# A two-block transformer kernel: the hybrid mixers' convolution tiles, value tiles and convolution norm in another order

## The reference, cut to what matters

```python
def hybrid_mixer(h, cos, sin, w_in, q_a_norm, w_uq, kv_a_norm, w_ukv, conv_w,
                 attn_out_norm, conv_out_norm, w_o):
    proj = h @ w_in          # 1024 -> 384 + 256 + 32 + 512 + 512 + 512
    c_q, c_kv, k_pe, gate_b, gate_c, val = jnp.split(proj, offs, axis=-1)
    q = (rms_norm_2(c_q, q_a_norm) @ w_uq)      # 8 heads of 64 + 32 (rotated)
    kv = (rms_norm_2(c_kv, kv_a_norm) @ w_ukv)  # 8 heads of 64 keys + 64 values
    ...                                         # k_pe is rotated and shared by the heads
    attn = causal_attention(q_full, k_full, v)
    conv = gate_b * causal_short_conv(gate_c * val, conv_w)   # 3 taps along the tokens
    merged = concatenate([rms_norm_2(attn, attn_out_norm), rms_norm_2(conv, conv_out_norm)])
    return merged @ w_o
```

## Time and profile before

| what | value |
|---|---|
| median of three runs | 3661.96 us |
| the profiled execution's own time | 3659.31 us |
| its span, first to last instruction | 3657.5 us |
| mean granted TensorE clock | 0.989 of full speed |
| TensorE (PE) busy | 3585.8 us, 98% |
| VectorE (DVE) busy | 2027.3 us, 55% |
| ScalarE (ACT) busy | 1296.0 us, 35% |

### The profile page before, as it was taken

The page is one execution under the profiler, slowest core; times in us unless marked ns, Lnnn a source line. Parts: engine busy times, 40 slices in busy tenths (PEclk is TensorE's granted clock), DMA queues, the critical chain, the costliest instruction groups (busy, mean ns, idle before and its releaser), DMA issues. The chain is left out here.

```text
span 3657.5 us, 46530 instructions
## 1 busy us (share of the span) xinstructions
PE 3585.8 (98%) x17492; PEld 2883.4 (79%) x17492; DVE 2027.3 (55%) x3405; ACT 1296.0 (35%) x2116; POOL 57.2 (2%) x108
## 2 busy tenths in 40 slices
PE   8999999999999999999999998999999999989999
PEld 7777777888866788888888776888888887778887
DVE  5777776655766565575334656433443346564334
ACT  4545444222243332223233433322332234333232
POOL 0000000000000000000000000000000000000000
PEclk9999999999999999999999998999999999989999
DMA  4222212655511265552222211222222322212232
GB/s 140 73 73 76 73 62 104 217 177 198 173 58 47 81 214 187 185 196 91 95 96 93 78 62 58 91 98 98 92 92 98 98 92 69 70 52 94 95 99 81
DMA packets 141561, 386.22 MB, mean 106 GB/s; under 512 B 21424, under 2 KB 62768, under 8 KB 141392
## 3 DMA queue, kind: packets, MB, share of 16 engines
q1 hardware_dynamic: 126928, 306.39, 25.4%
q0 software_dynamic: 14464, 77.60, 6.2%
HBM read 381.85 MB, written 2.10 MB: 105 GB/s over the span
## 5 line engine op out<-in xcount | busy, mean ns | idle before, releaser
L1079 PE MATMUL psP<-h_hi,w_hi 128*128 128x512 f32 x2664 | 1061.3, 398 | 6.1 <-ACT h_hi L689 3.0
L1080 PE MATMUL psP<-h_hi,w_lo 128*128 128x512 f32 x2664 | 1038.9, 390 | 0.0
L1084 PE MATMUL psP<-h_lo,w_hi 128*128 128x512 f32 x2664 | 1028.8, 391 | 0.0
L1692 DVE TENSOR_TENSOR w_lo<-raw,w_hi 128x1024 fp32r<-128x1024 f32 (+1 forms) x465 | 557.8, 1200 | 378.4 <-ACT w_hi L649 371.8
L655 ACT ACTIVATE ybuf<-psP 128x512 f32<-128x512 f32 (+1 forms) x401 | 239.4, 597 | 1276.9 <-PE psP L1084 1276.4
L1079 PEld LDWEIGHTS psP<-h_hi,w_hi 128*128 128x128 f32 x2664 | 500.9, 188 | 135.7 <-issue 34.4
L1084 PEld LDWEIGHTS psP<-h_lo,w_hi 128*128 128x128 f32 x2664 | 498.7, 188 | 109.5 <-DVE h_lo L1773 5.0
L1080 PEld LDWEIGHTS psP<-h_hi,w_lo 128*128 128x128 f32 x2664 | 501.4, 188 | 101.2 <-issue 2.9
L1079 PE MATMUL psP<-a_hi,w_hi 128*128 128x512 f32 x1248 | 495.8, 397 | 3.4 <-DVE w_lo L1692 3.4
L649 ACT ACTIVATE w_hi<-raw 128x1024 fp32r<-128x1024 f32 (+1 forms) x465 | 480.4, 1033 | 37.3 <-PE psP L1084 37.3
L1080 PE MATMUL psP<-a_hi,w_lo 128*128 128x512 f32 x1248 | 487.5, 391 | 0.0
(11 more groups left out here) (320 smaller groups left out, 3597.4 us busy)
## 6 DMA issues: line engine op xcount, KB each, us to landing
raw<-in_gu SPq DMA_DIRECT2D x264, 512.0 KB, 3.3
adaw<-in_ada POOLq DMA_DIRECT2D x96, 768.0 KB, 5.0
raw<-in_down SPq DMA_DIRECT2D x96, 448.0 KB, 3.3
raw<-in_down SPq DMA_DIRECT2D x48, 512.0 KB, 3.5
raw<-in_qkv SPq DMA_DIRECT2D x40, 512.0 KB, 3.6
raw<-in_mix_in SPq DMA_DIRECT2D x34, 512.0 KB, 3.2
raw<-in_qkv SPq DMA_DIRECT2D x64, 256.0 KB, 3.0
raw<-in_wo SPq DMA_DIRECT2D x32, 512.0 KB, 3.3
```

The costliest lines, as they stand in the source:

```text
L1079: nc.tensor.matmul(psP[:, s, :], hi, rhs[0](kt), start=(n == 0), stop=False)
L1080: nc.tensor.matmul(psP[:, s, :], lo, rhs[0](kt), start=False, stop=False)
L1084: mm = nc.tensor.matmul(psP[:, s, :], w_hi[:, s, kt * P:kt * P + P], rhs[1](kt), start=False, stop=(n == K - 1))
L1692: v.tensor_tensor(w_lo[:, s, 0:cols], raw[:, s, 0:cols], w_hi[:, s, 0:cols].bitcast(F32), ALU.subtract)\
```

## The change

The convolution tiles are distributed over all eight heads (19, 11, 19, 11, 19, 11, 11, 8 steps), and the last gate_b tile is put behind the heads. The value tiles come before the key tiles on all engines; the softmax of block 0 stands among the key tiles. On ScalarE the copies of the rotated key rows come behind the value evacuations. The convolution's norm and its scaled tiles are put behind the heads: TensorE first takes the attention half of three output tiles (highs, lows), with the column sums inside, then the spread, then the convolution half.

```diff
@@ -70,15 +70,13 @@
 CONV = [(kind, k) for k in range(4) for kind in ("gate_c", "value", "gate_b")]
-HEAD_CONV = (0, 2, 5, 6, 8, 11, 12, 12)
-HEAD_TILES = [[("q", h + 1)] + CONV[HEAD_CONV[h]:HEAD_CONV[h + 1]] for h in range(7)] + [[]]
-HEAD_CHUNKS = [(3, 2, 2, 2, 2, 2, 3, 3), (3, 3, 3, 3, 3, 4, 4, 4), (3, 2, 1, 1, 1, 1, 1, 1)] * 2 + [(3, 0, 0, 0, 0, 0, 0, 0), (0,) * 8]
-HEAD_CHUNKS[5] = (3, 2, 2, 2, 2, 0, 0, 0)
-CONV_STEP = 22
-CONV_UNITS = {27: 1, 28: 1, 29: 1, 30: 1}
-MIXER = [("c", m) for m in range(5)] + [("pe", 0), ("q", 0)] + [("K", j) for j in range(4)] + [("V", b) for b in range(4)]
+HEAD_CONV = (0, 2, 3, 5, 6, 8, 9, 10, 11)
+HEAD_TILES = [[("q", h + 1)] * (h < 7) + CONV[HEAD_CONV[h]:HEAD_CONV[h + 1]] for h in range(8)]
+HEAD_CHUNKS = [(3, 2, 2, 2, 2, 2, 3, 3), (3, 1, 1, 1, 1, 1, 1, 2)] * 3 + [(3, 1, 1, 1, 1, 1, 1, 2), (1,) * 8]
+MIXER = [("c", m) for m in range(5)] + [("pe", 0), ("q", 0)] + [("V", b) for b in range(4)] + [("K", j) for j in range(4)]
 for _tiles_of_head in HEAD_TILES:
     MIXER += _tiles_of_head
+MIXER += CONV[11:]
 K_STEP, V_STEP = MIXER.index(("K", 0)), MIXER.index(("V", 0))
@@ -975,16 +973,29 @@
                 evac()
-                prep(V_STEP, early=3)
+                prep(K_STEP, early=3)
+                def values(b):
+                    if b == 0:
+                        act.wait_ge(N_ckv.rstd_ready, N_ckv.turns(l) + 1)
+                    act.wait_ge(tile_done, pos.count(RING + 1))
+                    nc.scalar.activation(v_all[:, b, :], psP[:, pos.slot(), :], copy, scale=small[:, 1, 2, b:b + 1]).then_inc(evac_done, 1)
+                    pos.step()
+                values(0)
+                values(1)
+                act.wait_ge(N_ckv.bc_ready, N_ckv.turns(l) + 1)
+                nc.scalar.activation(key_scale[:, :], psS[:, 1, T:2 * T], copy).then_inc(key_scale_ready, 1)
+                values(2)
+                values(3)
                 act.wait_ge(kpe_ready, 3 * l + 1)
...
                 nc.scalar.activation(k_late[64:96, :, :], pe_rows.broadcast_to((32, 4, T)), copy).then_inc(kpe_ready, 2)
-                act.wait_ge(N_ckv.bc_ready, N_ckv.turns(l) + 1)
-                nc.scalar.activation(key_scale[:, :], psS[:, 1, T:2 * T], copy).then_inc(key_scale_ready, 1)
-                for j in range(4):
-                    pos.step()
-                prep(V_STEP + 4, early=6)
+                prep(K_STEP + 4, early=6)
+                prep(K_STEP + 5, early=3)
                 def exp2(n):
@@ -1019,42 +1030,32 @@
-                def values(b):
-                    if b == 0:
-                        act.wait_ge(evac_done, pos.count(RING))
-                        act.wait_ge(N_ckv.rstd_ready, N_ckv.turns(l) + 1)
-                    act.wait_ge(tile_done, pos.count(RING + 1))
-                    nc.scalar.activation(v_all[:, b, :], psP[:, pos.slot(), :], copy, scale=small[:, 1, 2, b:b + 1]).then_inc(evac_done, 1)
+                for j in range(4):
                     pos.step()
-                values(0)
-                values(1)
                 exp2(0)
-                values(2)
-                prep(V_STEP + 5, early=3)
                 exp2(1)
                 turned(0)
-                values(3)
-                prep(V_STEP + 6)
+                act.wait_ge(evac_done, pos.count(RING))
+                prep(K_STEP + 6)
                 for n in range(32):
...
                     finish(h, 2 * i)
-                    if n == CONV_STEP + 1:
-                        rstd_by_log(N_co)
                     if n + 1 < 32:
...
                     finish(h, 2 * i + 1)
-                    if 0 <= n - CONV_STEP - 3 < 4:
-                        conv_hi(n - CONV_STEP - 3)
                     if n >= 30:
...
                 attn_hi(3)
+                evac()
+                prep(pos.n - first + 2)
+                rstd_by_log(N_co)
+                for m in range(4):
+                    conv_hi(m)
                 for a, s in enumerate(lands):
@@ -1540,10 +1541,10 @@
                 tile(3, cq_split, before=q_tile_at)
-                spread(N_ckv, l, psS[:, 1, T:2 * T])
                 consumed2(4)
-                s = pos.slot()
-                for j in range(4):
+                def keys(s, j):
                     slot_ready()
@@ -1613,24 +1614,19 @@
                 s = pos.slot()
-                scores(0)
                 values(s, 0)
                 values(s, 1)
+                spread(N_ckv, l, psS[:, 1, T:2 * T])
+                values(s, 2)
+                values(s, 3)
+                s = pos.slot()
+                keys(s, 0)
+                keys(s, 1)
+                scores(0)
+                keys(s, 2)
                 scores(1)
-                values(s, 2)
+                keys(s, 3)
                 turn(0)
-                values(s, 3)
-                conv_units = iter([(kt, a) for a in range(3) for kt in range(4, KT)])
-                def conv_half(count):
-                    for _ in range(count):
-                        kt, a = next(conv_units)
-                        if kt == 4:
-                            slot_ready(a)
-                        pe.wait_ge(N_co.h_ready, N_co.turns(l) * 4 + kt - 3)
-                        highs(a_split, kt - 4, kt, pos.slot(a))
-                        lows(2 * KT, a_split, kt - 4, kt, pos.slot(a))
@@ -1648,28 +1644,38 @@
                     fill(h, 2 * i)
-                    if n == CONV_STEP + 1:
-                        stats(N_co, l, acc, psS[:, 1, T:2 * T])
                     if n + 1 < 32:
...
                     fill(h, 2 * i + 1)
-                    conv_half(CONV_UNITS.get(n, 0))
                     weigh(n)
-                    if n == CONV_STEP + 2:
-                        spread(N_co, l, psS[:, 1, T:2 * T])
-                    elif n >= 29:
+                    if n >= 29:
                         turn_out(n - 29)
-                conv_half(6)
-                turn_out(3)
-                conv_half(2)
+                tile(KT, h_split, beside={7: [lambda: turn_out(3)]})
                 pe.wait_ge(ao_hi, l * 4 + 4)
                 for a in range(3):
+                    slot_ready(a)
                     for kt in range(4):
-                        highs(a_split, 4, kt, pos.slot(a))
-                pe.wait_ge(ao_ready, l * 4 + 4)
+                        highs(a_split, kt, kt, pos.slot(a))
+                    if a == 0:
+                        pe.wait_ge(ao_ready, l * 4 + 4)
+                    if a == 1:
+                        stats(N_co, l, acc, psS[:, 1, T:2 * T])
+                    for kt in range(4):
+                        lows(2 * KT, a_split, kt, kt, pos.slot(a))
+                spread(N_co, l, psS[:, 1, T:2 * T])
+                def conv_half(kt, a):
+                    pe.wait_ge(N_co.hi_ready, N_co.turns(l) * 4 + kt - 3)
+                    highs(a_split, kt, kt, pos.slot(a))
+                    pe.wait_ge(N_co.h_ready, N_co.turns(l) * 4 + kt - 3)
+                    lows(KT, a_split, kt, kt, pos.slot(a))
+                for kt in (4, 5):
+                    for a in range(3):
+                        conv_half(kt, a)
                 for a in range(3):
-                    for kt in range(4):
-                        lows(KT, a_split, 4 + kt, kt, pos.slot(a))
+                    for kt in (6, 7):
+                        conv_half(kt, a)
                 for a in range(3):
@@ -2297,7 +2303,11 @@
                 query(0)
-                prep(V_STEP)
+                v.memset(spare[:, 5:6], 0.0).then_inc(y_used, 8)
+                prep(K_STEP)
+                for b in range(4):
+                    pos.step()
+                dve.wait_ge(evac_done, pos.count(RING))
                 for j in range(4):
@@ -2306,7 +2316,6 @@
                     pos.step()
-                v.memset(spare[:, 5:6], 0.0).then_inc(y_used, 8)
@@ -2408,13 +2417,11 @@
+                prep(K_STEP + 4)
+                prep(K_STEP + 5)
                 masked(0)
-                for b in range(4):
-                    pos.step()
-                prep(V_STEP + 4)
                 masked(1)
-                prep(V_STEP + 5)
-                prep(V_STEP + 6)
+                prep(K_STEP + 6)
                 for n in range(32):
@@ -2423,15 +2430,8 @@
                     finish(h, 2 * i + 1)
-                    m = n - CONV_STEP - 3
-                    if m == -2:
-                        variance(N_co, l, 512, psS[:, 1, T:2 * T], False)
-                    elif m == -1:
-                        rstd_by_log(N_co)
-                    elif 0 <= m < 4:
-                        conv_scaled(m)
-                        squares_before(m)
-                        conv_lo(m)
+                    if 24 <= n < 28:
+                        squares_before(n - 24)
                     if n >= 30:
@@ -2442,6 +2442,15 @@
                 attn_lo(3)
+                gate_b(3)
+                prep(pos.n - first + 2)
+                variance(N_co, l, 512, psS[:, 1, T:2 * T], False)
```

(6 more changed lines are left out.)

## The result

The changed kernel takes 3673.17 us (median of 13 runs, 3666.28 to 3678.01) against 3661.38 for the kernel before (13 runs in the same rounds, 3658.02 to 3665.82). The ratio is 1.0028, 95% interval 1.002 to 1.0037: slower by 0.28%, 11.8 us. The direction was as forecast and the range held the time, but the forecast, 3684, had put the loss (22 us over the median of before that it knew) at about twice its size. The profiled execution took 3667.92 us, span 3666.1, mean granted clock 0.994; that of before 3659.31, 3657.5 and 0.989. So profile to profile the loss is only 8.6 us: the profiled execution lies at the lower end of the new kernel's runs.

A forecast was written before the change was run, and what follows sets the result against it. TensorE, busy 98%, was taken as the bound, changeable only through waits and lower clock. Losses of 44.0 us a mixer less 32.1 gave 11.9 more, 23.8 in two, hence 3684 us, range 3655 to 3704.

The forecast's parts named there:

- The start: Mixer's first tiles, values ahead of keys: waits of 1.4 and 4.2 us plus 2.0 lower clock, 7.6 against 2.3.
- The waits of the light heads: Eleven-step heads 1, 3, 5 and 6: TensorE waits 3.4 us each for a 12.5 us VectorE and ScalarE queue.
- The waits of the tail: Head 7 and behind, through output transposes, spread and fourth output tile: 9.0 us of TensorE waits a mixer.
- The clock: TensorE's lower clock after waits: 2.3 us in each of heads 1, 3, 5, 6, 2.0 at the start, 3 from head 7.
- head 2's loss: Eleven-step head 2 of the kernel before: 5.0 us lost, 2.7 of it waiting and 2.3 the lower clock.
- the losses that I counted for before: TensorE's waits and lower-clock time in the kernel before, summed over start, heads and tail: 32.1 us a mixer.
- the 12.9 us that I had as its ideal: Ideal length of an eleven-step head: 5.2 us of attention work plus 0.70 us a step.
- heads 2 and 4: Nineteen-step heads of the changed kernel, taken to repeat the old head 3: 0.5 us lost in each.
- Rival 1: Spreading covers the heads: heads 1, 3, 5 and 6 lose no more than 0.5 us each; 3640 us, chance 0.14.
- Rival 2: The clock stays up: eleven-step heads and the start wait but are not slowed; 3661 us, chance 0.10.
- Rival 3: The clock stays low from head 5 or 6 to the end; 3702 us, chance 0.16.
- Rival 4: Tail waits of 2.0 and 2.5 us come out as zero and the clock stays up there; 3669 us, chance 0.12.

The follow-up runs named there:

- e_defer: Changed kernel with VectorE's split of the next weights moved behind the next mask in heads 1, 3, 5 and 6; 3655.28 us against 3659.33 before, 0.9987.
- e_act: Changed kernel with only ScalarE's copy of the next weights' high part moved behind the turned probabilities' copy in heads 1, 3, 5, 6; 3677.9 us, 1.0046 against before.
- e_start_old: Changed kernel with the old start order, key tiles ahead of value tiles, on all engines; 3661.93 us against 3659.33 for the kernel before, ratio 1.0008.
- e_start_alone: Kernel before with only the new start, value tiles ahead of key tiles; 3667.99 us against 3659.33 for the kernel before, ratio 1.0029.
- e_front: Changed kernel with the eleven steps of heads 1, 3, 5 and 6 moved toward each head's front; 3643.32 us against 3659.33 for the kernel before, 0.9958.
- e_combo: Changed kernel with old start, eleven-step heads' steps moved to the front and VectorE's split behind the next mask; 3625.58 us against 3659.59 before, 0.9908.
- the first four experiments: The runs e_start_old, e_start_alone, e_defer and e_front, each compared with the kernel before at 3659.33 us.
- e_warm: Changed kernel with small unused matmuls added ahead of the two waiting transposes of heads 1, 3, 5 and 6; 3663.29 us against 3659.59 before, 1.0008.

## Why the prediction was half right

**The start: right.** Forecast 1.4 and 4.2 us; measured, in time order:

```profile
2078.96 0.46 PE L1578 MATMUL psS<-k_early,q 96*128 96x128 f32 x2 [1.38 <-ACT k_late L995]
...
2086.78 0.33 PE L1589 MATMUL psS<-ident,prob 128*128 128x128 f32 x1 [4.13 <-ACT prob L1005]
```

VectorE's chain behind the last key tile is what was named, two evictions and the splits of both weights ahead of the first mask:

```profile
2083.38 0.69 DVE L2317 TENSOR_TENSOR k_late<-psP,on 64x512 f32<-64x512 f32 x1
2084.11 1.69 DVE L2265 TENSOR_TENSOR w_lo<-raw,w_hi 128x384 fp32r<-128x384 f32 x2
2085.84 0.35 DVE L2348 CUSTOM_DVE_ANT_0 prob<-psS,mask,qscale 128x128 f32<-128x128 f32 x1
```

The clock behind it, 2.0 forecast, cost 1.7 and 2.6 in the new kernel's two mixers and 1.5 to 3.2 in those of the kernels that share its start. Its weight in the whole I had not seen: 7.6 - 2.3 = 5.3 a mixer, 10.6 in two, and it measured 8.7 alone.

**The waits of the light heads: right.** 3.4 us a head forecast, 3.3, 3.2 and 3.2 measured in heads 1, 3 and 5; head 6, 4.0 against 3.7. The second wait of each ends with VectorE's queue, as e_defer shows, and ScalarE's copy has no part in it, as e_act shows.

**The waits of the tail: too dear.** Of 9.0 forecast, 5.8 came. The first weighing 0.99 instead of 1.5, the output transposes 2.5 instead of 4.3, the spread's 1.50 instead of 2.0, the fourth output tile 0.77 for 0.7:

```profile
2237.49 0.66 PE L1613 MATMUL psS<-ident,on 128*128 128x128 f32 x4 [1.85 <-DVE on L2396]
...
2250.17 0.50 PE L1080 MATMUL psP<-a_hi,w_hi 128*128 128x512 f32 x1 [1.50 <-ACT a_hi L1031]
```

**The clock: the step that failed.** "I take the same 2.3 for the clock: 5.7" priced a fall behind every light head, 2.0 behind the start and 3 in the tail, 14.2 us a mixer. Measured: 5.1 and 10.8, a mean of 8.0: 2.1 behind the start, 5.0 behind the light heads (forecast 9.2) and 0.9 in the tail (forecast 3). Two things were wrong in it. One is the size: a fall behind heads 3 and 5 costs 1.7, not 2.3 (behind head 6 of the second mixer it lasted twice as long and cost 3.1). The 2.3 was what was left of head 2's loss after its waits; the earlier trace rows's own clock of 0.90 over 17.9 us comes to 1.8. The other is the certainty: both mixers of the kernel before had shown a fall behind the 1.95 wait, and I took two for a rule. Over the four kernels whose light heads (or head 2) keep that wait of 1.95 to 1.97, a fall followed in 10 of 16 cases (before 2 of 2, after 4 of 6, e_start_old 4 of 6, e_start_alone 0 of 2). Head 6 of after and e_start_old, with a wait of 2.54, had one in 3 of 4. What decides which of such waits get one, the runs don't show. The Trainium skill, "TensorE: Matmul & The Clock Gate", section "HAM oscillation", tells of a loop whose waits last some 3 to 5 us and which pays the return to full speed anew in every round; the traces agree for the 4.1 us of the start (12 of 12, in the six kernels that have it), while behind the 2 us of the heads it was paid only in part of the cases.

**What the sum had under a wrong name, or not at all.** Against the losses that I counted for before, 32.1 us, the table has 29.5 and 31.1. And the new kernel's "rest" is 2.2 us a mixer higher. A light head takes more than the 12.9 us that I had as its ideal even where it neither waits nor is slowed: head 1 is busy 13.86 us at clock 1.00. In head 2 of before some 0.6 of this hid in the 2.3 that I called clock. A likely reason, argued and not shown: with 18 more filled chunks TensorE changes more often between attention's small instructions and the projection's, which would be about 0.1 us each time. e_front, with eight filled chunks fewer, gives 0.4 to 1.0 back, which fits but doesn't isolate it; no run measured the change of work by itself. The full account of a mixer: forecast 28.8 of waits, 14.2 of clock and 1.0 in heads 2 and 4, which measured nothing, less 32.1: +11.9; measured (mean of the two) +7.7 of waits, -5.2 of clock and +2.2 of rest, +4.7. Of the 7.2 between them the clock is 6.2, the waits 4.0 (3.2 of them in the tail) and heads 2 and 4 1.0; the losses of before (1.8) and the rest (2.2) go the other way. So the forecast came as near as it did in part because errors cancelled.

**The rivals.** Rival 1 didn't happen, but its condition pointed the right way: with the queue a split shorter (e_defer, 4 us under before) or three more steps of work ahead of the wait (e_front, 16 under), the new kernel beats before, though its start still costs 9. The Trainium skill, "Perfetto Trace Analysis", section "Optimization Strategy", has it that interleaving regimes with different busiest engines may gain; here the new distribution with the old start brought nothing (e_start_old, 1.0008), and 0.92% once the queue was covered (e_combo). Rival 2 holds in part: no fall in 6 cases of 16 in the heads, but one at every start. Rival 3 was wrong: heads 6 and 7 ran at clock 1.00 in the mixer above, and in the second the fall of head 6 was over before head 7. Rival 4's tail came out with waits of a third less than forecast, not with none; the clock there stayed up in one of the two mixers.

## What to carry to other kernels

When steps are spread evenly over attention heads, check every head for the in-order queue of the second engine (here 12.5 us, most of it on VectorE) against TensorE's work in front of the wait; a split or copy that nobody needs soon goes behind the mask, and the steps go to the front of the head. The order of the tiles and the queue have to be changed together: with the old start, the new order of the heads and the norm alone brought +2.6 us, which can't be told from nothing, and -34 with the two edits to the queue and the chunks. Price a wait of some 2 us by its length and, for the clock behind it, by how often such a fall occurs over many like places, not by the two that one trace shows.

## What the runs showed that I hadn't expected

The same wait in the same place is followed by the lower clock in one mixer and not in the other mixer of the same execution (heads 3 and 1 of e_start_old, for one). The spread between runs goes with the mean granted clock: among the new kernel's 13 runs the time goes from 3668 us at a mean granted clock of 0.994 to 3677 at 0.989, and among the 24 of before beside the first four experiments from 3654 to 3657 at 0.992 to 0.994 to 3660 to 3663 at 0.987 and 0.988. Where the falls in the heads are gone the spread is smaller, 4.0 us over 11 runs of e_defer and 8.6 over 11 of e_warm against 11.7 over 13 of the new kernel. A single profile of such a kernel can mislead: the new kernel's was 5 us under its median.

Waits of 1.4 us and less in the light heads were never followed by a fall in e_front and e_defer (eight heads each, the longest wait 1.41). That is no bound: behind the waits of 1.2 us in head 5 (for acc) and in the tail of before a fall came in both mixers. Small matmuls of unused result, some 0.55 us each (the "rest" of e_warm's mixers is 18.7 us higher for 34 of them), put into the gaps, kept the clock up in every head and were worth some 8 us.
